# Head norms inside the latent layers' projections, and the first stream's masked keys on VectorE

## The reference, cut to what matters

```
(na_q, na_k, na_v, gl_q, gl_k, gl_v, gl_g, gl_lr, ga_q, ga_k, ga_v) = split(u @ w_in)     # and the same for uc
o_na = neighborhood_attention(na_q, na_k, na_v, ..., rpb)                                   # 6 heads
o_gl = gla_bidirectional(gl_q, gl_k, gl_v, gates(gl_lr), ...)                               # 4 heads, two directions ("streams")
q_ga = apply_axial_rope(rms_norm_2(ga_q, q_norm_w), cos, sin)                               # 6 heads of 64
k_ga = apply_axial_rope(rms_norm_2(ga_k, k_norm_w), cos, sin)                               # 2 heads of 64
o_ga = gqa_latent_attention(q_ga, k_ga, ga_v, ...)                                          # context keys: norm, no rope
```

## Time and profile before

| what | us |
|---|---|
| median of 3 runs (2460.0 to 2465.69) | 2463.52 |
| the profiled execution's own time | 2463.47 |
| its span, first to last instruction | 2461.7 |
| TensorE busy in it (mean granted clock 0.979) | 2294.4 |
| VectorE / ScalarE / GpSimd busy | 950.9 / 641.0 / 134.5 |
| layer 0: joint stage | 1350.8 to 1433.9 |
| layer 1: joint stage | 2086.0 to 2150.9 |

### The profile page before, as it was taken

The page is one execution under the profiler, slowest core; times in us unless marked ns, Lnnn a source line. Parts: engine busy times, 40 slices in busy tenths (PEclk is TensorE's granted clock), DMA queues, the critical chain, the costliest instruction groups (busy, mean ns, idle before and its releaser), DMA issues. The chain is left out here.

```text
span 2461.7 us, 34225 instructions
## 1 busy us (share of the span) xinstructions
PE 2294.4 (93%) x14016; PEld 1490.0 (61%) x14016; DVE 950.9 (39%) x1762; ACT 641.0 (26%) x1031; POOL 134.5 (5%) x145
## 2 busy tenths in 40 slices
PE   6998999999999999999899888999999999889998
PEld 4866533334444344443487555678888878558997
DVE  2345321122111111111221766654343452757654
ACT  2434100001000000100142444342121253345433
POOL 0010000000000000000000223200000200211001
PEclk9989999999999999999999999999999999899999
DMA  9567699999999999999833533232332324435652
GB/s 304 171 205 262 253 405 429 427 429 427 429 429 428 429 428 429 428 428 428 335 106 113 167 125 112 78 100 67 116 103 77 103 77 142 154 121 137 184 169 93
DMA packets 264156, 606.02 MB, mean 246 GB/s; under 512 B 9808, under 2 KB 227920, under 8 KB 239344
## 3 DMA queue, kind: packets, MB, share of 16 engines
q1 hardware_dynamic: 264048, 604.48, 64.9%
HBM read 603.39 MB, written 1.05 MB: 246 GB/s over the span
## 5 line engine op out<-in xcount | busy, mean ns | idle before, releaser
L2014 PE MATMUL banks<-moe_ring,moe_x 128*64 128x512 f32 (+1 forms) x1920 | 349.6, 609 | 43.0 <-DMA moe_ring<-in_w_mlp 43.0
L2014 PEld LDWEIGHTS banks<-moe_ring,moe_x 128*64 128x64 f32 (+1 forms) x1920 | 117.2, 129 | 264.1 <-issue 263.2
L2226 DVE SCALAR_TENSOR_TENSOR res<-banks,mod,res 128x256 f32<-128x256 f32 x136 | 59.5, 479 | 519.7 <-PE banks L2035 501.8
L2577 PE MATMUL banks<-ff_xhi,ff_whi 128*128 128x512 f32 (+1 forms) x704 | 238.2, 338 | 7.1 <-DVE ff_xlo L2476 6.4
L2577 PE MATMUL banks<-ff_xhi,ff_wlo 128*128 128x512 f32 (+1 forms) x704 | 237.1, 337 | 0.0
L2577 PE MATMUL banks<-ff_xlo,ff_whi 128*128 128x512 f32 (+1 forms) x704 | 237.0, 337 | 0.0
L566 DVE TENSOR_TENSOR ff_wlo<-ring,ff_whi 128x2048 fp32r<-128x2048 f32 (+2 forms) x72 | 152.1, 2112 | 97.2 <-ACT ff_whi L557 94.8
L2119 ACT COPY moe_x<-banks 128x256 f32<-128x256 f32 x68 | 25.4, 373 | 595.3 <-PE banks L1974 595.3
L557 ACT CAST ff_whi<-ring 128x2048 fp32r<-128x2048 f32 (+2 forms) x72 | 126.5, 1757 | 124.8 <-PE banks L2609 118.3
L2577 PEld LDWEIGHTS banks<-ff_xhi,ff_whi 128*128 128x128 f32 x704 | 134.0, 190 | 23.7 <-DVE ff_xlo L2476 6.2
L2577 PEld LDWEIGHTS banks<-ff_xlo,ff_whi 128*128 128x128 f32 x704 | 133.9, 190 | 14.0
(11 more groups left out here) (443 smaller groups left out, 3579.4 us busy)
## 6 DMA issues: line engine op xcount, KB each, us to landing
moe_ring<-in_w_mlp SPq DMA_DIRECT2D x128, 2048.0 KB, 17.0
ring<-in_w_mlp SPq DMA_DIRECT2D x64, 2048.0 KB, 15.7
ring<-in_w_ada SPq DMA_DIRECT2D x144, 512.0 KB, 4.7
ring<-in_w_ffn_in SPq DMA_DIRECT2D x88, 512.0 KB, 5.0
ring<-in_w_in SPq DMA_DIRECT2D x60, 512.0 KB, 4.6
ring<-in_w_out SPq DMA_DIRECT2D x24, 512.0 KB, 4.4
ring<-in_w_ffn_out SPq DMA_DIRECT2D x32, 384.0 KB, 3.1
ring<-in_w_ffn_out SPq DMA_DIRECT2D x16, 512.0 KB, 4.5
```

Of the source, the lines that this page charges most:

```text
L2014: mm = nc.tensor.matmul(u_bank[o][c:c + n_cols, :], x[:, 2 * kk + r, c:c + n_cols], self.moe_piece(2 * kk + m)[:, at:at + 512], start=Fals ...
L2226: return nc.vector.scalar_tensor_tensor(r, source, self.mod[:, 5, d, 0:1], r, ALU.mult, ALU.add)
L2577: mm = nc.tensor.matmul(bank[:, 0:width], w[:, k, :], xp[:, k, :], start=(k == 0 and term == 0), stop=(k == KC - 1 and term == 2))
```

## The change: what it does

The first part: `layout` and the order in which the weights are loaded put `wide(2)` and `wide(3)` first and `wide(0)` and `wide(1)` last. So `ga_q` and `ga_k` are in `b_tok` after four of the eleven chunks, and the norms become turns of `project`: VectorE takes two of them behind the low half of chunks 5, 6, 8, 9 and 10, ScalarE its Ln and Exp in chunk 7. The scratch `nn_sq` is gone; chunk 0 of `h`, which has been read by then, takes its place. The second part: `kept_keys` yields between its four products, takes the engine as an argument, and in the joint stage runs on VectorE in turns 3, 4, 6 and 7 of the gates. In stage 4 it stays on GpSimd. In the diff below the lines with `norms` are `project`'s, `NORMED` is 5, the `pool` lines are GpSimd's and the last ones VectorE's turns in the joint stage.

```
-IN2 = [[(0, 512)], [(512, 512)], [(1152, 256)], [(1664, 256)], [(1920, 128)],
-       [(1024, 128), (1408, 256), (1952, 128)], [(2080, 512)]]
+IN2 = [[(1024, 128), (1408, 256), (1952, 128)], [(2080, 512)], [(1152, 256)], [(1664, 256)], [(1920, 128)],
+       [(0, 512)], [(512, 512)]]
-                layout = wide(0) + wide(1) + two(0, 1, width, 2 * S) + two(2, 3, width, width)
-                layout += [(0, KC, [(0, P, "feat", 4, 0, 2 * S)])] + wide(2) + wide(3)
+                layout = wide(2) + wide(3) + two(0, 1, width, 2 * S) + two(2, 3, width, width)
+                layout += [(0, KC, [(0, P, "feat", 4, 0, 2 * S)])] + wide(0) + wide(1)
...
+                    if norms and i == NORMED + 2:
+                        self.norms_scalar(act, self.cond[:, 0:4, 0:8])
...
+                    if norms and i >= NORMED and i != NORMED + 2:
+                        next(turns, None)
+                        next(turns, None)
...
+            dve.wait_ge(self.sums_taken.sem, self.sums_taken.at(5 + t))
...
-                    for slot in range(n_gates):
-                        if slot == 6:
-                            pool.wait_ge(self.loaded, self.n_loaded)
-                            pool.wait_ge(self.dup_ready.sem, self.dup_ready.at(1))
-                            self.kept_keys(first, keys, k2, levels)
...
+                    masked = self.kept_keys(nc.vector, first, keys, k2, levels)
+                        if slot == 3:
+                            dve.wait_ge(self.dup_ready.sem, self.dup_ready.at(1))
+                        if slot in (3, 4, 6, 7):
+                            next(masked)
```

More of the change, by code:

```diff
@@ L59 @@
 PASSES = (((0, 6), (6, 11)),) * 2, (((0, 8), (8, 16), (16, 22)),)
+NORMED = 5
 SLOTS = 4
@@ L778, in input_low, with project @@
                 .then_inc(self.xlo_ready.sem, self.xlo_ready.one())
-    def project(self, layout, width, tok, feat, clear=None, constants=None, head=None):
+    def project(self, layout, width, tok, feat, clear=None, constants=None, head=None, norms=None):
         nc = self.nc
@@ L875, in _ @@
                                      lambda dve: self.split_low(dve, bufs, n, 1, 2))
+                if norms:
+                    asking, l = norms
+                    flat = self.h[:, 0, :].rearrange("p (h d) -> p h d", d=HD)
+                    turns = self.norms_vector(dve, tok, flat, self.cond[:, 0:4, 0:8], asking, l)
                 for i in range(2 if head else 0, chunks):
@@ L879, in _ @@
                         self.input_low(dve, x, width)
+                    if norms and i >= NORMED and i != NORMED + 2:
+                        next(turns, None)
+                        next(turns, None)
+                if norms:
+                    for _ in turns:
+                        pass
             if clear:
@@ L2699, in _, with norms_vector @@
                 self.refill(sp, total)
-    def norms_vector(self, dve, tok, sq, rot, ms, asking, l):
+    def norms_vector(self, dve, tok, rot, ms, asking, l):
         nc, step = self.nc, self.dve_step
@@ L2707, in norms_vector @@
             own = slice(first(t), 8)
-            nc.vector.tensor_tensor(sq[:, own, :], heads(t)[:, own, :], heads(t)[:, own, :], ALU.mult)\
+            dve.wait_ge(self.sums_taken.sem, self.sums_taken.at(5 + t))
+            nc.vector.tensor_tensor(rot[:, own, :], heads(t)[:, own, :], heads(t)[:, own, :], ALU.mult)\
                 .then_inc(step.sem, step.one())
             dve.wait_ge(step.sem, step.count)
-            nc.vector.reduce_sum(ms[:, t, own], sq[:, own, :], AX_X).then_inc(step.sem, step.one())
+            nc.vector.reduce_sum(ms[:, t, own], rot[:, own, :], AX_X).then_inc(step.sem, step.one())
             dve.wait_ge(step.sem, step.count)
@@ L2716, in norms_vector @@
             yield
-        yield
-        yield
         dve.wait_ge(self.norms_rooted.sem, self.norms_rooted.at(1))
@@ L2751, in norms_scalar @@
     def norms_scalar(self, act, ms):
-        for _ in range(5):
-            yield
         act.wait_ge(self.norms_summed.sem, self.norms_summed.at(1))
-        m = ms[:, :, :]
+        m = ms
         self.nc.scalar.activation(m, m, ACT.Ln).then_inc(self.act_step.sem, self.act_step.one())
@@ L2758, in norms_scalar @@
         self.nc.scalar.activation(m, m, ACT.Exp, scale=-0.5).then_inc(self.norms_rooted.sem, self.norms_rooted.one())
-        while True:
-            yield
     def window_and_gates(self, l, v, steps, gq, gk, gg, lr, wa, tok, cum, near, tau, q2, k2, keys, state, levels,
@@ L2775, in window_and_gates @@
         halves = 2 * (len(steps) + 2)
-        n_norms, n_gates, n_side = 11, 20, 4 * side["chunks"] + 1
+        n_gates, n_side = 20, 4 * side["chunks"] + 1
         with ExitStack() as ctx, self.stage() as block:
             bufs = self.pair_buffers(f"b2a{l}", ctx)
-            sq = self.sb("nn_sq", [P, 8, HD], ctx=ctx)
-            rot, ms = sq, self.cond[:, 0:4, 0:8]
             gate = self.sb("gl_gate", [P, 2, 2 * S], ctx=ctx)
@@ L2793, in _ @@
             def _(pool):
-                def gates():
-                    for slot in range(n_gates):
-                        if slot == 6:
-                            pool.wait_ge(self.loaded, self.n_loaded)
-                            pool.wait_ge(self.dup_ready.sem, self.dup_ready.at(1))
-                            self.kept_keys(first, keys, k2, levels)
-                        yield
-                self.alternate((self.pairs_pool(pool, steps, bufs), halves), (gates(), n_gates))
-                pool.wait_ge(self.keys_kept.sem, self.keys_kept.at(1))
+                for _ in self.pairs_pool(pool, steps, bufs):
+                    pass
             @block.tensor
@@ L2877, in gates @@
                         yield
-                self.alternate((self.pairs_scalar(act, steps, bufs), halves), (self.norms_scalar(act, ms), n_norms),
-                               (gates(), n_gates), (self.sides_scalar(act, side), n_side))
+                self.alternate((self.pairs_scalar(act, steps, bufs), halves), (gates(), n_gates), (self.sides_scalar(act, side), n_side))
             @block.vector
@@ L2947, in _, with kept_keys @@
                 self.alternate((self.pairs_vector(dve, steps, bufs, mask), halves),
-                               (self.norms_vector(dve, tok, sq, rot, ms, 2 * v, l), n_norms),
                                (gates(), n_gates), (self.sides_vector(dve, side), n_side))
-    def kept_keys(self, s, keys, k2, levels):
+    def kept_keys(self, eng, s, keys, k2, levels):
         fine = len(LEVELS) - len(COARSE)
         for t in range(2):
-            self.nc.gpsimd.tensor_scalar(keys[:, :, 0, P * t:P * t + P], k2[:, :, S * s + P * t:S * s + P * t + P],
+            eng.tensor_scalar(keys[:, :, 0, P * t:P * t + P], k2[:, :, S * s + P * t:S * s + P * t + P],
                                          self.tab("ways")[:, t:t + 1], None, ALU.mult)
@@ L2960, in kept_keys @@
             for c in range(2):
-                op = self.nc.gpsimd.tensor_tensor(
+                op = eng.tensor_tensor(
                     keys[:, c, i0:i1, :].rearrange("p i (t k) -> p i t k", k=P),
@@ L2964, in kept_keys @@
                     kept, ALU.mult)
-        op.then_inc(self.keys_kept.sem, self.keys_kept.one())
+                if i1 == 8 and c == 1:
+                    op.then_inc(self.keys_kept.sem, self.keys_kept.one())
+                yield
     def queries_and_streams(self, l, turns, streams, steps, gg, tok, cum, near, tau, q2, k2, keys, state, levels):
@@ L3258, in stream @@
                                 pool.wait_ge(self.sums_ready.sem, self.sums_ready.at((n_sets + 2) * (y + 1)))
-                                self.kept_keys(streams[y + 1], keys, k2, levels)
+                                for _ in self.kept_keys(nc.gpsimd, streams[y + 1], keys, k2, levels):
+                                    pass
                             own_decays(streams[y + 1], slot - 14)
@@ L3324, in constants @@
                               self.dram["levels"].rearrange("p (m t) -> p m t", t=P))
-                self.project(layout, 2 * S, tok, feat, clear, constants, head)
+                self.project(layout, 2 * S, tok, feat, clear, constants, head, (2 * v, l))
                 state = self.sb("gl_state", [P, 2, P], ctx=ctx)
```

## The result

The changed kernel takes 2444.33 us (median of 5 runs, 2441.28 to 2453.41) against 2462.35 (5 runs, 2460.00 to 2465.69): 0.9933 of the time, 95% interval 0.9919 to 0.9947, some 18 us less by the medians, 16.5 by the ratio; 2447 was forecast. The profiled execution took 2441.28, 3 us under its median, with a span of 2439.5.

What follows compares the result with a forecast made beforehand. TensorE itself bounds the projections; in the joint stages VectorE's list ends most of its waits. Joint stages -8.0 and -7.4, order -1.5, last copy +0.2: -16.7 us on 2463.47, so 2447 us, range 2440 to 2456.

Steps and rivals of the forecast that it cites:

- The projections pay nothing: Projections: the dearest turn of norms, some 4 us, fits VectorE's estimated 5.4 us of idle time, so TensorE never waits.
- Rival D: Projections: norms collide with the low halves and give back the joint stages' gain, 2463 us; chance 0.03.
- The order, -1.5 in layer 1: Layer 1's projection: wider first chunks fill TensorE's 4.4 us of input waits with later work, gaining 1.5 us.
- The keys' price, 4.9 us: Joint stages: the key scalings and products cost VectorE 4.9 us per layer.
- B: Joint stages: keys cost VectorE what they cost GpSimd, 6.6 us more per layer; no change, 2460 us; chance 0.06.
- The 4.5 us of slow-down go with the keys: Layer 0's joint stage: `stat`, mask and square lose 4.5 us of excess once GpSimd's key products leave.
- without the excess and the square `line` comes 4.8 us earlier: Layer 0's joint stage: from `stat` to `line` 4.7 us instead of 9.55, gaining 4.2 us of TensorE's waits.
- The waits: Joint stages: TensorE's waits for `line` in layer 0 fall from 5.2 to about 2 us, `gl_gate` to near 0.
- The clock, -1.6 and -3.0: Joint stages: low-clock stretches behind shortened waits vanish, gaining 1.6 us in layer 0 and 3.0 in layer 1.
- Rival A: Joint stages: TensorE runs into the next late thing, the chain with ScalarE; only half the gain, 2455 us; chance 0.17.
- C: Layer 1's joint stage: the clock stays low for more of TensorE's work; slower, 2471 us; chance 0.03.
- nothing later in the program starts from another engine's state: Stages after the changed ones: they start as before, so the whole 16.7 us gain carries through.

Runs made afterwards that it cites:

- e5: Changed kernel plus six more 512-element VectorE products behind each turn of norms in both layers' projections; 2444.11 us, ratio 0.9916 to the kernel before.
- e3: Kernel before with only the keys moved to VectorE in four turns, old chunk order and norms kept; 2459.50 us, ratio 0.9985.
- e2: Kernel before with the new order and the norms in the projection, joint-stage keys still on GpSimd; 2446.86 us, ratio 0.9933.
- e9: The same kernel as e2, run again beside the changed kernel on one chip; 2447.01 us, ratio 0.9934 to the kernel before.
- e8: The changed kernel run once more, nothing altered; 2446.96 us, ratio 0.9932 to the kernel before.
- e1: Kernel before with only the new order of chunks in the latent projections; 2458.09 us, ratio 0.9992.
- e6: Changed kernel with five instead of three filler products ahead of the first stream scores in layer 1's stage behind the joint one; 2440.04 us.
- e10: e6 with three more filler products in layer 1's joint stage ahead of the gates' products; 2439.02 us, ratio 0.9909 to the kernel before.

## Why the prediction was right, and where not

**The projections pay nothing: right.** 504 products, no wait for `pr_wlo`. At the tight place the turn took 4.08 us (2031.36 to 2035.44) and 1.35 were left, together the 5.4 that were estimated. That the cover ends there was wrong on the safe side (e5). Rival D is out: turns twice as long cost one wait of 1.4 us.

**The order, -1.5 in layer 1: mis-sized.** The waits fell by 1.6 as put; the stage gained 2.8, because the lower clock behind them (0.98 over the stage before) went as well. That term was missing. It is no chance of one profile: both profiles with the old order (before, e3) have 0.98 and 100.0 to 100.1 us, all with the new one 1.00, and 97.3 but for e5's wait.

**The keys' price, 4.9 us: right** (0.95 and 1.22 for each product), so B is out.

**The 4.5 us of slow-down go with the keys: right as a fact, but most of the gain didn't need it.** By the Trainium skill, "SBUF — State Buffer", section "Who interferes with whom", operations with two inputs in SBUF contend with GpSimd's reads and reductions don't. The traces agree: `stat` and the mask are slow beside GpSimd in e2 (2.55, 1.63) as in the earlier trace rows, and the two peaks, one input each, are not, in e2 (1.28) or before:

```profile
1379.16 1.27 DVE L1259 TENSOR_REDUCE b2a_peak<-banks 128x1 f32<-128x512 f32 x2
```

The reduction of 0.69 that the prediction names doesn't show this: behind that square it began at 1384.78, and GpSimd's products had ended at 1384.19. The step "without the excess and the square `line` comes 4.8 us earlier" put two cures into one term. With the norms gone 2.3 and 3.0 us of slow-down are left (e2, e9) and reach TensorE with 1.3 and 2.0; with the slow-down gone and the norms there, 3.6 come back in layer 0 and 0.3 in layer 1. Of the 18 us by the medians the norms with their order carry 15 to 17 (e2, e9), the keys alone 2.6, and on top of the norms nothing that the timed runs can tell from none.

**The waits: right.** `line` 1.4 us in layer 0 (about 2 forecast), `gl_gate` none. Without the clock, layer 0 was to gain 6.4 and gained 6.9 and 7.9 in its two profiles; layer 1 4.4, and gained 4.2 and 4.5.

**The clock, -1.6 and -3.0: right in the first profile, not reliable as terms.** They took the low stretches of one profile for consequences of the waits in it. Layer 0's held in four of the five profiles of this stage, but e8, with the same waits, is 4.6 us longer there, by the clock, and has 0.79 again at the place in layer 1 that was counted out. The Trainium skill, "TensorE: Matmul & The Clock Gate", section "What's actually happening", says that how long a kernel stays at the lower level at its start varies from run to run; e8 beside the first profile shows the same for stretches in the middle of a program. What could have been forecast is a mean and a spread: in layer 0's joint stage the two kernels that leave it alone lost 1.7 and 3.4 us (before, e1), the changed list nothing in four profiles and some 5 in one. What sets the fall here stays open.

The total is right in part by luck. Without the clock's two terms 12.1 us were forecast, and the stages gained 14 to 15 (6.9 to 7.9, 4.2 to 4.5, and the projection's 2.8 with its own clock). That leaves 1.5 to 4 of the 16.5 to 18 timed us, for which 4.6 of clock had been put; that it is the clock isn't shown.

**Rival A didn't come:** no wait on ScalarE grew; **C** neither, though its place was near: layer 1's stage behind the joint one gave back 2.9 us in the first profile, by the clock. So the step "nothing later in the program starts from another engine's state" didn't hold in that profile; e6 and e10 have the stage at the length of before with fillers, e2 and e5 without.

## What to carry to other kernels

When an engine that others wait for has a slow-down and a long list, try shortening the list first: work moved into a stage where that engine idles was worth the whole change here, as far as the timed runs tell, and half of the slow-down left with the work that it had struck. Where two edits both end the same wait, price each alone, or the credit goes to the one that looks more striking in the trace. Take a low clock in one profile as one draw until a second profile shows it: compare stage lengths times clock, and forecast the clock as a spread.

## What the runs showed of the hardware

One list of TensorE, with its waits in the stage equal to the tenth, took 74.07 us in the changed kernel's first profile and 78.63 in e8. The difference lies in stretches at the lower clock, one of which began 14 us after TensorE's last idle time. Beside GpSimd's key products VectorE's two-input operation on 1024 elements took 2.55 us (e2) and 3.28 (e9) instead of 1.23, while a pair of reductions took 1.28 in e2 and in the changed kernel. VectorE needs less than half of GpSimd's time for the same four products (4.3 for 9.63 us).
